# A four-branch diffusion trunk on one core: the third branch's merge products spread over the levels of a triangular inverse

## What is computed

```python
mod = silu(cond) @ ada_w + ada_b                 # (1024) x (1024, 6144): 24 slabs of 1 MB
sh1, sc1, g1, sh2, sc2, g2 = split(mod, 6)
h = rmsnorm(x) * (1 + sc1) + sh1
proj = h @ w_in                                  # every branch's inputs, its gates, and merge (4 x 1024)
y_a, y_b, y_c, y_d = hyena(..), hgrn2(..), ssd(..), gated_deltanet(..)       # each 384 x 512
lifted = einsum("blnc,ncd->blnd", branches, w_branch)
mixed  = einsum("blnd,blnd->bld", sigmoid(merge), lifted)
x = x + g1 * (mixed @ w_out)
x = x + g2 * moe(rmsnorm(x) * (1 + sc2) + sh2)   # 64 experts, top 8, and a shared one
return rmsnorm(x)                                # and the final states of three branches
```

## Time and profile before

| | us |
|---|---|
| median of 3 runs | 1379.75 (1378.31 to 1380.78) |
| the profiled execution's own time | 1378.36 |
| its span in the profile | 1376.2 |
| PE busy in the span | 1327.2 (96%) |
| DVE, ACT, POOL busy | 604.7, 378.9, 307.2 |
| from the first modulation slab of group 1 to the fourth branch's first lift | 523.4 to 699.5 |

### The profile page before, as it was taken

One profiled execution on the slowest core, in us unless ns is written; L12 is line 12 of the kernel. 1 busy time (PEld: TensorE's weight loads), 2 busy tenths in 40 slices (PEclk: granted clock), 3 DMA queues, 4 the chain that ended last, 5 costly groups with the idle time before them and its releaser, 6 DMA issues.

```text
span 1376.2 us, 20641 instructions
## 1 busy us (share of the span) xinstructions
PE 1327.2 (96%) x7692; PEld 925.8 (67%) x7692; DVE 604.7 (44%) x1363; ACT 378.9 (28%) x765; POOL 307.2 (22%) x247
## 2 busy tenths in 40 slices
PE   7999999999999998799999999999999999999996
PEld 2695899989988996588988875444544445444452
DVE  3467452886545486643232375222233323222224
ACT  3232222322544254323311241211222112211122
POOL 0431234243135553332442010000000000000001
PEclk9999999999999999999999999999999999999998
DMA  9640423133212337712335247999999999999992
GB/s 364 215 126 10 138 93 123 33 121 93 92 61 93 107 123 276 261 42 82 113 104 195 93 168 268 419 418 420 419 421 421 420 421 421 421 419 419 419 416 82
DMA packets 109744, 321.57 MB, mean 234 GB/s; under 512 B 12489, under 2 KB 72649, under 8 KB 81136
## 3 DMA queue, kind: packets, MB, share of 16 engines
q1 hardware_dynamic: 98416, 307.68, 58.4%
q0 software_dynamic: 2560, 8.81, 1.6%
q10 hardware_dynamic: 8704, 4.20, 1.1%
HBM read 320.11 MB, written 4.33 MB: 236 GB/s over the span
## 4 chain that ended last, share of the span: by engine, by line
PE 85%; DMA 9%; DVE 3%; issue 1%; ACT 1%; SPq 0%; POOL 0%; DVEq 0%; POOLq 0%; ACTq 0%
PE banks L660 24%; PE banks L627 17%; PE banks L3051 12%; DMA w<-in_exp_w 7%; PE banks L3098 7%; PE banks L2953 6%; PE banks L1067 2%; PE banks L2938 2%; PE banks L1236 2%; PE banks L2946 1%; PE banks L900 1%; PE banks L634 1%; PE banks L779 1%; PE banks L711 1%; PE banks L1295 1%
## 5 line engine op out<-in xcount | busy, mean ns | idle before, releaser
L3051 PE MATMUL banks<-w,xg 128*64 128x512 f32 (+1 forms) x1312 | 236.0, 594 | 2.1 <-DMA w<-in_exp_w 2.0
L3051 PEld LDWEIGHTS banks<-w,xg 128*64 128x64 f32 (+1 forms) x1312 | 71.9, 126 | 151.5 <-issue 125.3
L660 PE MATMUL banks<-hT,ring 128*128 128x192 f32 x888 | 154.4, 326 | 0.2 <-DMA ring<-in_w_in 0.2
L660 PEld LDWEIGHTS banks<-hT,ring 128*128 128x128 f32 x888 | 145.5, 190 | 2.8 <-DMA ring<-in_w_in 0.9
L3428 POOL DMA_INDIRECT fetched<-token_rows,row_of_place x32 | 32.1, 1004 | 443.6 <-DVE row_of_place L3229 433.5
L3098 PE MATMUL banks<-w,hidT 128*64 128x512 f32 (+1 forms) x656 | 122.8, 601 | 0.5 <-DMA w<-in_exp_w 0.3
L2953 PE MATMUL banks<-y,selT 128*128 128x512 f32 x384 | 115.0, 415 | 0.0
L660 PE MATMUL banks<-x,ring 128*128 128x192 f32 x592 | 108.8, 327 | 2.7 <-POOL ring L2582 1.7
L660 PE MATMUL banks<-x,combos 128*128 128x192 f32 x592 | 108.4, 326 | 0.7 <-ACT yT L1407 0.7
L660 PEld LDWEIGHTS banks<-x,ring 128*128 128x128 f32 x592 | 97.4, 190 | 3.4 <-issue 2.0
L660 PEld LDWEIGHTS banks<-x,combos 128*128 128x128 f32 x592 | 98.1, 190 | 1.0 <-POOL ring L2598 0.9
(11 more groups left out here) (513 smaller groups left out, 1946.2 us busy)
## 6 DMA issues: line engine op xcount, KB each, us to landing
w<-in_exp_w SPq DMA_DIRECT2D x198, 1024.0 KB, 14.0
ring<-in_w_in SPq DMA_DIRECT2D x46, 1024.0 KB, 5.4
ring<-in_ada_w SPq DMA_DIRECT2D x24, 1024.0 KB, 6.0
ring<-in_w_branch SPq DMA_DIRECT2D x8, 1024.0 KB, 5.4
ring<-in_w_out SPq DMA_DIRECT2D x4, 1024.0 KB, 6.8
arena<-in_sh_w SPq DMA_DIRECT2D x3, 1024.0 KB, 8.0
x<-in_x_sample SPq DMA_DIRECT2D x4, 512.0 KB, 8.4
token_rows<-whole_rows SPq DMA_DIRECT2D x3, 384.0 KB, 21.7
```

The source lines that it names most:

```text
L660: last = mm(out, lhsT=w[:, k, :], rhs=tokens[:, k, :], start=start and k == 0, stop=k == KD // 2 - 1, skip_group_check=not start)
L3051: ins = mm(ps[lo:hi, :], lhsT=xg[:, k, a_ * P + lo:a_ * P + hi], rhs=w13[:, a_, u, :, k, :], start=k == 0, stop=k == KD - 1)
```

## The change

The pieces of work and their sizes stay the same. What moves:

- The third branch's merge products (2, 0) to (2, 3) and its eight lifts, which began at `(1, 5)`, now begin at "start" and stand one by one in the small levels and at every point of the later levels. The modulation slabs, which stood one at each point of the small levels, are spread out to the end of the stage.
- `combine` of a merge product, which POOL did at the `close` of the product before it, is an entry of its own. A point `(r, 6)` gets an AFTER list too.
- The slabs of this stage are loaded in the new order of use, and a table `OWN_SLOT` gives each its place in the ring, in place of the plain rotation. Merge slabs stay at place 3, the two lift slabs at place 2, modulation slabs mostly at 0 and 1.
- ACT's wait ahead of storing the gate rows is for modulation group 1 instead of 2; the two small DVE steps that make `mod_parts`, and PE's wait for them, stand later.

```diff
         DELTA_FILL = {
-            "start": (("ada", 1, 3, 5), ("q_norms",), ("values",)),
-            ("c", 1): (("ada", 1, 5, 6),),
-            ("c", 2): (("ada", 1, 7, 8),),
-            ("c", 3): (("ada", 2, 1, 2),),
-            ("c", 4): (("ada", 2, 3, 4),),
-            (0, 5): (("ada", 2, 5, 6),),
-            (0, 6): (("ada", 2, 6, 8), ("scaled_values",), ("combine", 2, 0)),
-            (1, 5): (("ada_columns", 2), ("open", 2, 0), ("residual", 0, FWD), ("residual", 0, BWD)),
-            (1, 6): (("solve", 1, FWD), ("lift", 0), ("lift", 1), ("open", 2, 1)),
-            (2, 5): (("state", FWD), ("close", 2, 1)),
-            (2, 6): (("open", 2, 2), ("solve", 2, FWD), ("solve", 2, BWD)),
-            "end": (("close", 2, 2), ("state", BWD), ("lift", 4), ("lift", 5), ("residual", 1, BWD), ("open", 2, 3),
-                    ("query_rows",), ("close", 2, 3), ("solve", 1, BWD), ("lift", 6), ("lift", 7), ("combine_gate", 0),
-                    ("open_gate", 0), ("solve", 0, FWD), ("solve", 0, BWD), ("close_gate", 0), ("out", 1), ("open_gate", 1),
-                    ("out", 2), ("close_gate", 1), ("out", 0), ("last_state",), ("combine", 3, 0), ("open", 3, 0),
-                    ("turn", 1), ("turn", 2), ("close", 3, 0), ("turn", 0))}
+            "start": (("combine", 2, 0), ("q_norms",), ("values",), ("ada", 1, 3, 4), ("open", 2, 0)),
+            ("c", 1): (("ada", 1, 4, 5), ("close", 2, 0)),
+            ("c", 2): (("lift", 1),),
+            ("c", 3): (("open", 2, 1),),
+            ("c", 4): (("lift", 2),),
+            (0, 5): (("open", 2, 2),),
+            (0, 6): (("lift", 4), ("scaled_values",)),
+            (1, 5): (("residual", 0, FWD), ("residual", 0, BWD), ("combine", 2, 3), ("lift", 5)),
+            (1, 6): (("solve", 1, FWD), ("open", 2, 3)),
+            (2, 5): (("state", FWD), ("close", 2, 3), ("lift", 6)),
+            (2, 6): (("solve", 2, FWD), ("solve", 2, BWD), ("combine_gate", 0), ("ada", 2, 4, 5)),
+            "end": (("state", BWD), ("ada", 2, 5, 6), ("open_gate", 0), ("residual", 1, BWD), ("close_gate", 0), ("ada", 2, 6, 7),
+                    ("query_rows",), ("solve", 1, BWD), ("ada", 2, 7, 8), ("solve", 0, FWD), ("solve", 0, BWD), ("ada_columns", 2),
+                    ("open_gate", 1), ("out", 1), ("close_gate", 1),
+                    ("out", 2), ("combine", 3, 0), ("open", 3, 0), ("out", 0), ("last_state",), ("turn", 1), ("turn", 2),
+                    ("close", 3, 0), ("combine", 3, 1), ("turn", 0))}
         DELTA_AFTER = {
-            ("c", 1): (("ada", 1, 6, 7),),
-            ("c", 2): (("ada_columns", 1), ("ada", 2, 0, 1)),
-            ("c", 3): (("ada", 2, 2, 3),),
-            ("c", 4): (("ada", 2, 4, 5),),
-            (0, 5): (("keys_to_end",),),
-            (1, 5): (("close", 2, 0),),
-            (2, 5): (("lift", 2), ("lift", 3), ("residual", 1, FWD))}
+            ("c", 1): (("lift", 0),),
+            ("c", 2): (("combine", 2, 1), ("ada", 1, 5, 7)),
+            ("c", 3): (("ada", 1, 7, 8), ("close", 2, 1)),
+            ("c", 4): (("combine", 2, 2), ("lift", 3), ("ada_columns", 1), ("ada", 2, 0, 1)),
+            (0, 5): (("keys_to_end",), ("close", 2, 2)),
+            (0, 6): (("ada", 2, 1, 2),),
+            (1, 5): (("ada", 2, 2, 3),),
+            (1, 6): (("ada", 2, 3, 4),),
+            (2, 5): (("lift", 7), ("residual", 1, FWD))}
...
+        plan_ada(1, 0, 3)
+        plan_merge(2, 0)
+        plan_ada(1, 3, 5)
+        plan_branch(2, 0)
+        plan_merge(2, 1)
+        plan_ada(1, 5, 8)
+        plan_ada(2, 0, 1)
+        plan_merge(2, 2)
+        plan_ada(2, 1, 2)
+        plan_branch(2, 1)
+        plan_ada(2, 2, 4)
+        plan_merge(2, 3)
+        plan_ada(2, 4, 6)
+        plan("gdn_g", 1)
+        plan_ada(2, 6, 8)
+        plan("gdn_g", 2, 1)
         plan_lift(3)
...
+        OWN_SLOT = dict(zip([name for name, _ in slab_plan[slab_at["ada", 1, 0]:slab_at["gdn_g", 1] + 1]],
+                            (0, 1, 2, 3, 0, 1, 2, 3, 0, 1, 0, 1, 3, 0, 2, 1, 0, 3, 1, 0, 3, 1, 0, 2)))
+        base = slab_at["ada", 1, 0]
+        slot_of, use_of, before_in_slot, loads_in = [], [], [], [[] for _ in range(SLABS)]
+        for i, (name, _) in enumerate(slab_plan):
+            q = (base + OWN_SLOT[name]) % SLABS if name in OWN_SLOT else (slot_of[-1] + 1) % SLABS if i else 0
+            slot_of.append(q)
+            use_of.append(len(loads_in[q]))
+            before_in_slot.append(loads_in[q][-1] if loads_in[q] else None)
+            loads_in[q].append(i)
...
                     name, src = slab_plan[i]
-                    if i >= SLABS:
-                        sp.wait_ge(*slab_last[i - SLABS])
+                    if before_in_slot[i] is not None:
+                        sp.wait_ge(*slab_last[before_in_slot[i]])
...
-            pe.wait_ge(s_row_parts.sem, 1)
             lift(3, 0, 2, merged=True)
...
-                    banks.emptied(act, ("adaT", 2))
+                    banks.emptied(act, ("adaT", 1))
...
-                    elif what == "close" and j[1] < 3:
-                        combine("merge", j[0], j[1] + 1)
```

More of the change, by code:

```diff
@@ L534, in trunk, with plan_ada, plan @@
         slab_plan = []
-        def plan_ada(group):
-            for k in range(KD):
+        def plan_ada(group, lo=0, hi=KD):
+            for k in range(lo, hi):
                 slab_plan.append((("ada", group, k), ada[k * P:(k + 1) * P, None, group * 2048:(group + 1) * 2048]))
         plan_ada(0)
-        def plan(name, halves=2):
-            for h in range(halves):
+        def plan(name, halves=2, first=0):
+            for h in range(first, halves):
                 slab_plan.append(((name, h), cols_of(w_in, COL[name] + h * 256)))
@@ L546, in plan_merge, with plan_branch @@
             slab_plan.append((("merge", n, h), cols_of(w_in, COL["merge"] + n * D + h * 256)))
+        def plan_branch(n, h):
+            slab_plan.append((("wb", n, h), a["w_branch"][0, n][:, h * W:h * W + W].rearrange("(k p) n -> p k n", p=P)))
         def plan_lift(n, first=0):
@@ L552, in plan_lift @@
                 if h % 2 == 0:
-                    slab_plan.append((("wb", n, h // 2), a["w_branch"][0, n][:, h // 2 * W:h // 2 * W + W]
-                                      .rearrange("(k p) n -> p k n", p=P)))
+                    plan_branch(n, h // 2)
         for name in ("hy_v", "hy_x1", "hy_x2"):
@@ L576, in trunk @@
         slab_last = {}
+        OWN_SLOT = dict(zip([name for name, _ in slab_plan[slab_at["ada", 1, 0]:slab_at["gdn_g", 1] + 1]],
[8 more added lines that the diff above has]
+            loads_in[q].append(i)
         def slab(pe, name, kd=KD):
             i = slab_at[name]
-            pe.wait_ge(s_slab[i % SLABS].sem, 16 * (i // SLABS + 1))
-            return ring[:, i % SLABS, :].rearrange("p (k n) -> p k n", k=kd)
+            pe.wait_ge(s_slab[slot_of[i]].sem, 16 * (use_of[i] + 1))
+            return ring[:, slot_of[i], :].rearrange("p (k n) -> p k n", k=kd)
         def blocks(name):
-            w = ring[:, slab_at[name] % SLABS, :].rearrange("p (k n) -> p k n", k=KD)
+            w = ring[:, slot_of[slab_at[name]], :].rearrange("p (k n) -> p k n", k=KD)
             return [[w[:, j * 4:j * 4 + 4, i * P:(i + 1) * P] for j in range(2)] for i in range(2)]
@@ L1213, in _ @@
                         per_head(("ginvT", r, l), "dve", lambda h: (gprod[:, h, :], gmix[:, h * P:(h + 1) * P]))
+                        fill((r, l), DELTA_AFTER)
             fill("end")
-            pe.wait_ge(s_row_parts.sem, 1)
             lift(3, 0, 2, merged=True)
@@ L1220, in _ @@
                 lift(3, 2 * h, 2 * h + 2, merged=True)
+            pe.wait_ge(s_row_parts.sem, 1)
             pe.wait_ge(s_madd.sem, 3 * KD - 2)
@@ L2470, in _ @@
                     banks.free(ins, key)
+            fill("end")
             lane.link(v.tensor_copy(mod_parts[:, 0], mod[:, 40:48, :]))
             s_row_parts.on(tt(mod_parts[:, 1], mod[:, 40:48, :], mod_parts[:, 0].bitcast(F32), ALU.subtract))
-            fill("end")
             lift(3, 0, 2)
@@ L2580, in combine @@
                 at = slab_at[name]
-                pool.wait_ge(s_slab[at % SLABS].sem, 16 * (at // SLABS + 1))
+                pool.wait_ge(s_slab[slot_of[at]].sem, 16 * (use_of[at] + 1))
                 s_combos.on(g.tensor_tensor(a21, a11, a21, ALU.subtract))
@@ L2724, in slabs @@
                     name, src = slab_plan[i]
-                    if i >= SLABS:
-                        sp.wait_ge(*slab_last[i - SLABS])
+                    if before_in_slot[i] is not None:
+                        sp.wait_ge(*slab_last[before_in_slot[i]])
                     n = src.shape[1]
-                    load(ring[:, i % SLABS, :].rearrange("p (k n) -> p k n", k=n), src, s_slab[i % SLABS])
+                    load(ring[:, slot_of[i], :].rearrange("p (k n) -> p k n", k=n), src, s_slab[slot_of[i]])
             load(first, a["t_first"], s_fnet)
```

4 lines of the change are left out of this document (removed).

## The result

The changed kernel takes 1372.41 us (median of 4 runs, 1370.68 to 1372.72) against 1380.26 us (median of 4 runs of the kernel before): a ratio of 0.9943, 95% interval 0.9926 to 0.996. It is 0.6% faster, which is about half of the forecast gain, and its time lies above the stated range. The profiled execution took 1372.2 us (span 1370.3) against 1378.36 (1376.2): 6.2 us less. I measure the rest by the **stage**, from the first modulation slab of group 1 to the first lift of branch 4, in single profiled executions. It took 176.11 us before and takes 169.86 us now. This removes what lies ahead of the stage, which differs by up to 2.1 us between the executions of this document, although no edit touches it.

What follows compares the result with a forecast made beforehand. PE, busy 96% of the span, bounds the kernel, and gains pass on completely. The stage loses 22.5 us now and 7.4 after, a gain of 15.1: 1364.7 us against the median, range 1360.5 to 1371.5, chance 0.62.

Steps and rivals of the forecast that it cites:

- `small_products(1)`: First small level: its half columns queue on ACT behind `keep`, so it finishes 0.5 us after `open` allows.
- the levels from the third on: Small levels c3 and c4: zero, thin; levels 5 and 6: idles of 0.3, 0.3 and 0.2 us.
- `open (2, 2)`: At c3 and c4: asks for ACT's first copy at 7.4 us, which comes at 7.0, so zero wait.
- a first wait for a bank: Before `open (2, 0)`: PE waits 3.2 us instead of 2.3 for the bank of the last query product.
- the two slabs behind merge slab (2, 1): Second small level: modulation slabs 1,5 and 1,6 queue behind this merge slab on SP; idle 1.7 us.
- Rivals 2, 3 and 4: 2: first wait and slabs free, 1361.5, 0.08; 3: ring starves PE, 1386.7, 0.04; 4: experts' stage returns gain, 1379.7, 0.04.
- Rival 1: Levels of the inverse: its chain gets slower and PE's fillers don't cover it; 1369.7 us, chance 0.22.
- the sum of what is lost after: Reordered stage: 3.2 + 0.5 + 1.7 + 0.3 + 0.3 + 0.2 + 1.2 = 7.4 us still lost, no slow stretch expected.
- Start: Opening of merge product (2, 0): idle 3.2 us for a bank DVE frees at 538.5, no slow clock behind.
- "Nothing on PE": Whole stage: the change adds or removes no work on PE, DVE or POOL; the slabs are the same 24.
- c2: Second small level: late modulation slabs idle PE 1.7 us, bounds 0 and 2.7.
- End: End of stage: the 1.73 us idle goes; the turned output before branch 4's first lift stays; 1.2 us lost.

Runs made afterwards that it cites:

- experiment 1: Changed kernel, but POOL's combination for merge product (2, 0) waits until DVE has placed the first level: 1369.43 us, ratio 0.9932.
- experiment 2: Changed kernel, but DVE weighs the last query product before it begins the first level's transposes: 1364.41 us, ratio 0.9892.
- experiment 4: Changed kernel, but the first three modulation slabs stand one by one between the key products: 1369.26 us, ratio 0.9935.
- experiment 8: Kernel of experiment 6, but POOL adds lift 5 before combining the weights of merge product (2, 3): 1362.55 us, ratio 0.9878.
- experiment 3: Changed kernel, but modulation slabs 1,5 and 1,6 are loaded ahead of merge slab (2, 1): 1369.57 us, ratio 0.9924.
- edits 2 and 3: Changed kernel with the edits of experiment 2 and experiment 3 together: 1362.49 us, ratio 0.9883.
- experiment 6: Kernel with edits 2 and 3, but modulation group 2's eight slabs stand in four blocks of two: 1364.73 us, ratio 0.9892.
- experiment 7: Kernel of experiment 6, with last states and third output ahead of opening merge product (3, 0), last turn ahead of its closing: 1362.36 us, ratio 0.9884.
- experiment 9: Kernel of experiment 6 with the edits of experiment 7 and experiment 8 together: 1362.26 us, ratio 0.9867.

## Why the prediction was off

Right in kind: the gain is PE idle time in the small levels, it is passed on 1 to 1 (5.79 us at the first lift and at the first expert load), and no later wait gives it back. What the filled levels were said to give was also right: `small_products(1)` waited 0.29 us (0.5 was said), the levels from the third on gave one idle, of 0.22 us (three, of 0.8 in all, were said), `open (2, 2)` did not wait, and a first wait for a bank and a wait for the two slabs behind merge slab (2, 1) came where they were foreseen. Rivals 2, 3 and 4 fell. Rival 1 was right that DVE's steps get slower beside POOL, and wrong on the place: it looked for that in each level's chain, and what cost PE time in the changed kernel stood ahead of a bank. Its time of 1369.7 was nearer than the forecast, but not by its own sum.

The step that failed is the sum of what is lost after, 7.4 us, in two of its terms above all: the first wait (3.2 us, its end taken as fixed, and no slow stretch behind it), and the work that the change adds on PE ("nothing"). Counted by starts, with one price for each kind of product, PE's pure work in the stage is 151.6 us in both traces. So 24.5 us were lost before (22.5 was taken) and 18.3 are lost after. Term by term:

- *Start*, forecast 3.2 us of idle and no window under the full clock: 4.8 and, behind it, 1.65 us at the lower clock. The walk took the end of the DVE row of 537.87 as fixed ("whose end does not move"). It moved, because POOL's new combination stretched the two predicated copies ahead of it by 1.94 us. The prediction weighed such collisions and checked L2429, L2437 and `add_up`; it passed over the predicated copies of which both inputs are in SBUF (L2419 before, L2446 now), and looked on the inverse's chain, not at who frees a bank. "SBUF — State Buffer" of the Trainium skill, "SBUF: two separate sides", says of the shared pair that "the other fully blocks"; 1.01 against 2.95 us, and experiment 1, agree. Without the collision (experiment 1) the idle is 2.83 us, close to the 3.2 forecast, and the stage 3.94 us shorter; leaving the wait out altogether (experiment 2) gives 6.68.
- *"Nothing on PE"*, forecast 0: changes between 32-column products (modulation slabs, small products) and full ones cost PE time that no bracket shows. The way in adds 93 ns to the last full product (205 instead of 112 ns, by starts), the way out 0.1 us or more and 0.1 at the next product; 0.33 us for a round trip in experiment 4, 0.36 in experiment 8. The old tables had slabs next to small products, the new ones put full products between: in the stage PE changes shape 17 times before and 35 times now, and by the same count 2.2 us were lost so before and 5.6 after, 3.4 more. "TensorEngine Tiling (Array Packing)" of the Trainium skill, Key Properties, has a reason that fits, without a price: "Mode switching requires drain". The runs show the cost, and not what happens in the array. The prediction did not weigh it.
- *c2*, forecast 1.7 us for the late slabs: 2.6 by experiment 3. Within the bounds given.
- *End*, forecast 1.2 us: the last idle, now 0.89, came as said. A second idle, of 0.67 us, where a half product waits for ACT's copy behind a root, has no term in the sum, though one of the same kind stood in the kernel before (0.66 us at 674.13). By starts it is 0.8 us.
- The turns of the values, which the sum doesn't have, lose some 0.4 us by starts, waiting for DVE (0.23 us in the bracket).

The forecast of 15.1 less the excess of 3.3 (start and its clock), 3.4 (switches), 0.9, 0.8 and 0.4 is 6.3 us; the stage gained 6.25. That it closes so well is partly luck: the terms that came out smaller than forecast (some 0.5 us in all) and small gaps that have no term (as much again) cancel. With edits 2 and 3, which take out the first and the third, the kernel is at 1362.49 us, below the 1364.7 that the prediction gave the change. This doesn't confirm its walk, as the edits also remove the 3.2 and 1.7 us that it had counted as lost.

What stays open: when the clock falls. Idles of 4.8 us were followed by a fall (two traces), those of 2.83 and 3.43 were not, and one of 2.22 was in experiment 6 and not in experiment 7. In the kernel before, the fall of the earlier trace rows came behind idles of 2.02 and 0.73 us, and none behind the 2.32 us at 536. In experiment 9 it fell at 837 us, where PE's idles in the 11 us before were 0.32 us at most. So the length of one idle alone does not tell, and no run shows what does. Each fall cost some 1.6 us here, which single executions have or don't have.

## What to carry to other kernels

Before moving work of one engine beside a chain on another, list every instruction near it that may share a resource, and also those that free a bank or a place, not the chain's steps alone; then move the new work by one position if it meets one. When filler is chosen for TensorE, put products of one array shape next to each other: here a gap filled with the other shape cost a third of a microsecond that no idle shows. And when idle time is counted from modelled ends, count the same stage once more by starts; the difference is where such costs hide.

## What the runs showed that I had not expected

- A DVE predicated copy of 128x192 with both inputs in SBUF: 1.01 us for two when POOL is quiet, 2.95 beside POOL's tensor_tensor. POOL is stretched too: in experiment 6 its steps took up to 1.72 us instead of 1.27.
- An earlier landing of a weight slab led to an idle of 2.22 us on PE (experiment 6), since it moved POOL's work onto DVE's.
- Between 32-column and full products, 93 ns by starts on the way in, whatever the full product's length: 205 for 112 (128 columns), 256 for 163 (192), 416 for 323 (384).
